# Evacuations after both halves of a split, one tile sum later, and an earlier turn in the mixer

## The chip, the cores and the metric

The kernel runs on one core of a Trainium2 chip. The metric is the device time of one launch in microseconds, and lower is better. The kernel before took 2287.01 us (median of 3 runs, 2286.39 to 2288.19).

The names of the engines in the profile: PE is TensorE (matmuls; PEld is its weight load), DVE is VectorE, ACT is ScalarE, POOL is GpSimd, SP is SyncE, which here only issues DMA transfers.

## The reference

A sequence of 256 tokens with 2048 features passes through two blocks, all in fp32. The part that fills most of the time is the MLP of the first block, which is computed twice, with other weights:

```python
for i in range(DEPTH):                     # DEPTH = 2
    h = rmsnorm(x, g[0])
    m = hyena_shortconv_mixer(h, ...) if i % 2 == 0 else pool_mixer(h, ...)
    x = x + rmsnorm(m, g[1])
    h = rmsnorm(x, g[2])
    f = jnp.square(jax.nn.relu(h @ mlp_w1[i])) @ mlp_w2[i]   # 2048 -> 8192 -> 2048
    x = x + rmsnorm(f, g[3])
```

The mixer of the first layer begins with `z = h @ w_in` (2048 by 6144, `in_w_z` in the trace). A third layer with three kinds of attention follows, and a last rmsnorm. The change doesn't touch it.

## The kernel before

**Products.** A weight tile is 128 by 2048 fp32 (1024 KB). A product of fp32 operands is made of three fp32r matmuls: each operand is split into a high part and the rest, and PE adds hi by hi, hi by low and low by hi into one PSUM bank (`product`, L353). The high part of a weight tile is an ACT copy (L497, `hi<-raw`), the low part a DVE subtraction (L616, `low<-raw,hi`). Each tile is split in two halves of 128 by 1024, so a tile costs ACT two copies and DVE two subtractions. PE waits for the low part of a tile's half before it begins that half's matmuls.

**Buffers.** There are 3 landing buffers (raw0 to raw2) and 3 pairs of operand buffers (hi and low, 0 to 2). SP loads tiles in the order in which they are used. A load waits until its landing buffer is free, and loads behind it on SP's queue wait as well.

**The order.** The order of all work is written out by hand: the function `conduct` runs once for each engine, and each engine keeps what is its own. Before a tile is used (`take`), the tiles up to two further on are split; after its last product (`release`) the one behind these, if an operand pair is free. `release` has an argument `between`, which is called between the two halves of that split. The evacuation of a finished PSUM bank is put there, so on ACT and DVE the order is: first half, evacuation, second half.

**The MLP.** A chunk is 1024 of the 8192 hidden features. The first goes up on its own; for each of the other 7 (e = 1 to 7, so 14 in both MLPs) `both_ways` interleaves the way up for chunk e with the way down for chunk e-1. The way up is done with 7 half-size products in place of 8 (a Strassen scheme in Winograd's form), each of 2 weight tiles: up(1) to up(7). The way down is 8 tiles of `w_d`, down(0) to down(7). A tile on the way up has 12 matmuls, one on the way down 24 (two banks). So a chunk is 22 tiles, in this order (numbers of the tiles in the chunk in brackets):

up(1) (0, 1), down(0) (2), up(2) (3, 4), down(1) (5), up(5) (6, 7), down(2) (8), up(3) (9, 10), down(3) (11), up(6) (12, 13), down(4) (14), up(7) (15, 16), down(5) (17), up(4) (18, 19), down(6) (20), down(7) (21).

**Tile sums.** The operands of the 7 products are sums of weight tiles. They are made in a chain in the buffers R_f and X (two tiles each). POOL issues accumulating DMAs into R_f (L1008), DVE adds two tiles with `tile_sum` (L601): `first_sum`, R_f<-R_f,X, and `third_sum(0)` and `third_sum(1)`, X<-X,raw. The third sums read the tiles of up(3) (9 and 10) where they have landed. They stand in the middle of down(2), and each also frees the landing buffer of its tile: only then does SP load the next tile of `w_d` into it. The buffer that third_sum(1) frees takes the tile of down(5), and the loads for down(6) and down(7) stand behind it on SP. X, the result, holds the tiles of up(7) (15 and 16).

**Evacuations in the MLP.** The end of up(6), `sixth`, is the long one: DVE combines two products (L601, `EV<-P,EV` twice, two banks), then ACT takes relu (L553) and square (L555) of the second. The ends of the odd down tiles add two banks to R_m on DVE (`summed`, L601, R_m<-P,R_m); for e = 1 they are copies on ACT.

**The mixer.** `gemm` computes 512 columns of `in_w_z` for two banks with 4 tiles. When one is done, the banks are evacuated to EV (ACT, L492), and four transposes on PE, a turn (L356, P<-ident,EV), bring a quarter of it into another layout. Turns stand in a list `later`, from which one entry is taken after each half tile; entries `nop` only put off what is behind them.

## Time and profile before

| | |
|---|---|
| median of 3 runs | 2287.01 us (2286.39 to 2288.19) |
| profiled execution, its time | 2288.19 us |
| its span in the trace | 2286.4 us |
| PE busy | 2265.3 us (99%), 10609 matmuls |
| PE weight load busy | 1874.1 us (82%) |
| DVE busy | 1724.9 us (75%) |
| ACT busy | 1325.8 us (58%) |
| POOL busy | 81.0 us (4%) |
| DMA | 513.26 MB, mean 224 GB/s |

The profiled execution is the slowest of the three. Its own time is 1.8 us over its span, 2288.19 less 2286.4, for what lies before the first and behind the last instruction. Idle time of an engine other than PE costs something only where PE waits for it. "Granted clock" or PEclk is the share of full speed that the throttle granted TensorE; 1.00 is 2.4 GHz.

### The profile page before, as it was taken

The numbers are of one execution on the slowest core, as the hardware profiler recorded it, in microseconds if no ns is written. First come the engines' busy times: TensorE is split into PE (matmuls) and PEld (weight loads), VectorE is DVE, ScalarE is ACT, GpSimd is POOL, SyncE is SP. The second block draws the span as 40 slices with busy tenths as digits, with TensorE's granted clock in tenths as the row PEclk, the third lists the DMA queues.
The fourth block names the chain that finished last, engine by engine and source line by source line (L and its number), as shares of the span: only waits on it lengthen the run. The fifth ranks groups of instructions, "written<-read, shape, count | busy, mean of one in ns | idle before, by whom it ended". The sixth has DMA issues, their size and how long they took to land.

```text
span 2286.4 us, 26583 instructions
## 1 busy us (share of the span) xinstructions
PE 2265.3 (99%) x10609; PEld 1874.1 (82%) x10609; DVE 1724.9 (75%) x2043; ACT 1325.8 (58%) x1769; POOL 81.0 (4%) x110
## 2 busy tenths in 40 slices
PE   9999999999999999999999999999999999999998
PEld 7778788878888888888887888888888888888887
DVE  6675864888788788887878888888878775456664
ACT  6444444666666766665666666666666564444453
POOL 0000000000000000000000000000000010000000
PEclk9999999999999999999999999999999999999999
DMA  9444455787797797786576797797688645654443
GB/s 351 168 165 169 160 187 184 272 242 226 256 283 236 251 282 229 258 265 239 224 288 188 247 286 219 242 290 223 241 272 239 232 159 200 246 187 148 147 157 120
DMA packets 73100, 513.26 MB, mean 224 GB/s; under 512 B 8234, under 2 KB 8565, under 8 KB 13520
## 3 DMA queue, kind: packets, MB, share of 16 engines
q1 hardware_dynamic: 61568, 429.58, 50.4%
q0 software_dynamic: 11264, 81.87, 16.0%
q8 instruction: 84, 1.38, 0.2%
q14 instruction: 40, 0.32, 0.0%
q10 hardware_dynamic: 144, 0.12, 0.0%
HBM read 505.24 MB, written 6.29 MB: 224 GB/s over the span
## 4 chain that ended last, share of the span: by engine, by line
PE 93%; DVE 3%; DMA 2%; ACT 1%; issue 1%; POOL 0%; SPq 0%; ACTq 0%; POOLq 0%; DVEq 0%
PE P L353 90%; PE P L356 3%; DVE low L616 2%; DMA raw<-in_w_d 1%; ACT hi L497 1%; DVE R_f L601 0%; DMA raw<-in_w_z 0%; DVE R_m L601 0%; DVE X L604 0%; DVE R_f_r L601 0%; ACT EV L523 0%; DVE R_h L604 0%; DVE R_g_r L601 0%; ACT R_m L492 0%; DVE st L604 0%
## 5 line engine op out<-in xcount | busy, mean ns | idle before, releaser
L616 DVE TENSOR_TENSOR low<-raw,hi 128x1024 fp32r<-128x1024 f32 (+3 forms) x694 | 813.2, 1199 | 281.8 <-ACT hi L497 277.6
L497 ACT ACTIVATE hi<-raw 128x1024 fp32r<-128x1024 f32 (+3 forms) x694 | 705.1, 1040 | 471.9 <-PE P L353 334.5
L353 PE MATMUL P<-hi,R_h 128*128 128x512 f32 (+2 forms) x2944 | 948.8, 394 | 1.7 <-DVE low L616 1.2
L353 PE MATMUL P<-hi,R_f_r 128*128 128x512 f32 x2480 | 793.7, 392 | 7.0 <-DVE low L616 6.7
L353 PEld LDWEIGHTS P<-hi,R_h 128*128 128x128 f32 x2944 | 553.3, 188 | 119.9 <-issue 8.6
L353 PE MATMUL P<-low,R_h 128*128 128x512 f32 (+2 forms) x1472 | 570.9, 388 | 0.0
L353 PEld LDWEIGHTS P<-hi,R_f_r 128*128 128x128 f32 x2480 | 467.2, 188 | 106.2 <-DVE low L616 8.0
L353 PE MATMUL P<-low,R_f_r 128*128 128x512 f32 x1240 | 484.0, 390 | 0.0
L353 PEld LDWEIGHTS P<-low,R_h 128*128 128x128 f32 x1472 | 277.2, 188 | 56.3 <-issue 4.3
L616 DVE TENSOR_TENSOR low<-R_f,hi 128x1024 fp32r<-128x1024 f32 x226 | 265.0, 1219 | 70.1 <-ACT hi L497 70.1
L353 PEld LDWEIGHTS P<-low,R_f_r 128*128 128x128 f32 x1240 | 233.6, 188 | 47.4
L497 ACT ACTIVATE hi<-R_f 128x1024 fp32r<-128x1024 f32 x226 | 230.7, 1052 | 60.0 <-PE P L353 30.2
L353 PE MATMUL P<-hi,R_g_r 128*128 128x512 f32 x448 | 142.4, 389 | 0.0
L553 ACT ACTIVATE EV<-EV,st 128x512 f32<-128x512 f32 x42 | 30.4, 724 | 120.8 <-DVE EV L601 120.8
L353 PEld LDWEIGHTS P<-hi,R_g_r 128*128 128x128 f32 x448 | 84.1, 188 | 17.4
L616 DVE TENSOR_TENSOR low<-X,hi 128x1024 fp32r<-128x1024 f32 x56 | 67.9, 1223 | 37.3 <-ACT hi L497 35.6
L353 PE MATMUL P<-low,R_g_r 128*128 128x512 f32 x224 | 87.1, 389 | 0.0
L1008 POOL DMA_DIRECT2D R_f<-in_w_u x56 | 48.6, 868 | 1013.0 <-DVE low L616 1013.0
L601 DVE TENSOR_TENSOR R_m<-P,R_m 128x512 f32<-128x512 f32 x112 | 71.9, 683 | 6.1 <-PE P L353 6.1
L353 PE MATMUL P<-hi,R_s_r 128*128 128x512 f32 x224 | 71.4, 390 | 0.0
L356 PE MATMUL P<-ident,EV 128*128 128x128 f32 (+1 forms) x476 | 66.4, 272 | 0.0
L497 ACT ACTIVATE hi<-X 128x1024 fp32r<-128x1024 f32 x56 | 58.8, 1057 | 11.4 <-PE P L353 11.4
(221 smaller groups left out, 1453.9 us busy)
## 6 DMA issues: line engine op xcount, KB each, us to landing
raw<-in_w_d SPq DMA_DIRECT2D x128, 1024.0 KB, 5.9
raw<-in_w_u SPq DMA_DIRECT2D x72, 1024.0 KB, 5.1
R_f<-in_w_u POOLq DMA_DIRECT2D x56, 1024.0 KB, 12.0
raw<-in_w_z SPq DMA_DIRECT2D x45, 1024.0 KB, 4.9
raw<-in_w_i SPq DMA_DIRECT2D x36, 1024.0 KB, 4.8
R_f<-in_w_u SPq DMA_DIRECT2D x28, 1024.0 KB, 6.6
X<-in_w_u SPq DMA_DIRECT2D x28, 1024.0 KB, 8.2
raw<-in_w_mo SPq DMA_DIRECT2D x16, 1024.0 KB, 4.9
```

Source lines behind the costliest of these rows:

```text
L353: return self.e.matmul(o, l, r, start=start, stop=stop, skip_group_check=True)
L356: return self.e.transpose(o, i, self.m.ident[0:i.shape[0], 0:i.shape[0]])
L497: self.e.activation(hi, raw, ACT.Copy).then_inc(*self.inc("high_made", ("high", k, d)))
L553: self.e.activation(o, p, ACT.Relu, scale=r).then_inc(*self.inc("act_done", evacuated))
L601: self.e.tensor_tensor(o, a, b, op).then_inc(*self.inc("dve_done", *done))
L616: self.e.tensor_tensor(low, raw, hi.bitcast(f32), ALU.subtract).then_inc(*self.inc("low_made", *lows))
L1008: self.e.dma_start(o, i, accum_op=ALU.add).then_inc(*self.landed(f"added{j}", done))
```

## The change

Three edits.

1. `between` is gone. `release` now splits both halves of the next tile and the evacuation comes behind them. The ends of up(6) and up(4) are called with `soon`, and there the evacuation comes first and both halves behind it.
2. `third_sum(1)` moves from the middle of down(2) to up(6), behind the `take` of its first tile (12). `third_sum(0)` stays.
3. In the mixer, the number of `nop` entries ahead of the turns of product 0 is 2 in place of 4, and none in place of 1 for product 1.

No instruction is added or removed. On SP and POOL the order of the instructions is the same in both kernels.

```diff
--- before.py
+++ after.py
@@ -1111,21 +1111,16 @@
 
     chain_last = [None] * 4
 
-    def split_ahead(n, between=None):
+    def split_ahead(n):
         while not listing and not at_["pause"] and at_["high"] < min(at_["load"], n):
             k = at_["high"]
             o = plan[k][7]
             if o is not None:
                 if o >= NO and o - NO not in used:
-                    break
+                    return
                 split_part(k, 0, 2)
-                if between is not None:
-                    between()
-                    between = None
                 split_part(k, 1, 2)
             at_["high"] += 1
-        if between is not None:
-            between()
 
     def quarters():
 
@@ -1160,7 +1155,7 @@
             return j, m.raw[l % NL][0:parts, 0:c]
         return j, m.hi[o % NO][0:parts, 0:c], m.low[o % NO][0:parts, 0:c]
 
-    def release(j, done, hold=False, between=None):
+    def release(j, done, hold=False):
         l, o = plan[j][6:8]
         if o is None:
             freed[l] = done
@@ -1168,7 +1163,7 @@
             used.add(o)
         load_ahead()
         if not hold:
-            split_ahead(j + 2 + AHEAD, between)
+            split_ahead(j + 2 + AHEAD)
 
 
     bank_free, bank_held = [[] for _ in range(8)], set()
@@ -1741,7 +1736,7 @@
         if n == 7:
             flush_all()
         ks, ms = evac(banks, done, scale_m=list(r1_m))
-        later += [nop] * {0: 4, 1: 1, 8: 1, 9: 1, 10: 1}.get(n, 0)
+        later += [nop] * {0: 2, 8: 1, 9: 1, 10: 1}.get(n, 0)
         for c in (0, 2):
             later.append(lambda kind=kind, c=c + 4 * (n % 2), ks=ks, ms=ms: mixer_turn(kind, c, ks, ms))
         if n == 7:
@@ -1863,7 +1858,7 @@
         def parts_of(n, *free):
             s_m[n] = plain_parts(SH[n], SL[n], SUM[n], [s_m[n], list(free)])
 
-        def half_product(b, xh, xl, ready, tiles, end, onto, aside):
+        def half_product(b, xh, xl, ready, tiles, end, soon, onto, aside):
 
             for n, tile in enumerate(tiles):
                 j, wh, wl = take(up_w, *tile)
@@ -1875,10 +1870,13 @@
                     whose = ([("product", j, 1)] if k == 3 else []) + ([("used", j, k // 2)] if k % 2 else [])
                     E.product(P[b][:, :], xh[:, 4 * n + k, :], xl[:, 4 * n + k, :], wh[:, k, :], wl[:, k, :], j, k,
                               onto is None and n == k == 0, n == 1 and k == 3, x, bank_free[b], *whose)
-                done = "product", j, 1
-                release(j, done, between=(lambda: end(b, done)) if n == 1 else None)
+                if n == 1 and soon:
+                    end(b, ("product", j, 1))
+                release(j, ("product", j, 1))
+                if n == 1 and not soon:
+                    end(b, ("product", j, 1))
                 step()
-            return done
+            return ("product", j, 1)
 
         def down_tile(e, i, banks, middle):
             g, q = i // 2, i % 2
@@ -1895,7 +1893,10 @@
                 if k == 1:
                     middle()
             done = ("product", j, 1)
-            release(j, done, between=(lambda: [summed(e, t, g, banks[t], done) for t in range(2)]) if q == 1 else None)
+            release(j, done)
+            if q == 1:
+                for t in range(2):
+                    summed(e, t, g, banks[t], done)
             step()
             return done
 
@@ -1970,8 +1971,8 @@
             h_left, h_right = list(h_m[0:8]), list(h_m[8:16])
             up_done = {}
 
-            def up(n, b, xh, xl, ready, tiles, end, onto=None, aside=nop):
-                up_done[n] = half_product(up_banks[b], xh, xl, ready, tiles, end, onto, aside)
+            def up(n, b, xh, xl, ready, tiles, end, soon=False, onto=None, aside=nop):
+                up_done[n] = half_product(up_banks[b], xh, xl, ready, tiles, end, soon, onto, aside)
 
             def down(i, middle=nop):
                 return down_tile(e - 1, i, down_banks, middle)
@@ -1984,14 +1985,14 @@
             up(2, 0, HH[:, HRIGHT, TOP], HL[:, HRIGHT, TOP], h_right, plain(b21), second, onto=ms[1], aside=lambda: first_sum(1))
             down(1)
             up(5, 1, SH[1], SL[1], s_m[1], linked(1), fifth)
-            down(2, lambda: [third_sum(j) for j in range(2)])
+            down(2, lambda: third_sum(0))
             up(3, 1, SH[4], SL[4], s_m[4], plain(b22, "kept"), third, onto=ms[5])
             down(3)
-            up(6, 0, SH[2], SL[2], s_m[2], linked(2), sixth)
+            up(6, 0, SH[2], SL[2], s_m[2], linked(2), sixth, True, aside=lambda: third_sum(1))
             down(4)
             up(7, 0, SH[3], SL[3], s_m[3], linked(4), seventh)
             down(5)
-            up(4, 1, HH[:, HRIGHT, BOTTOM], HL[:, HRIGHT, BOTTOM], h_right, linked(3), fourth)
+            up(4, 1, HH[:, HRIGHT, BOTTOM], HL[:, HRIGHT, BOTTOM], h_right, linked(3), fourth, True)
             left_free = down(6)
             right = [(c, *turned(c, right_ks(), right_ms())) for c in (4, 6)]
```

On DVE, in the middle of the first chunk, around down(2) (raw1 and raw2 in the rows with X hold tiles 9 and 10):

```order
 L616 TENSOR_TENSOR low1<-raw2,hi1 128x1024 x2
 L601 TENSOR_TENSOR X<-X,raw1 128x2048
-L601 TENSOR_TENSOR X<-X,raw2 128x2048
 L616 TENSOR_TENSOR low2<-raw0,hi2 128x1024 x2
 L616 TENSOR_TENSOR low0<-R_f,hi0 128x1024 x2
```

The second sum has left this place; the first is where it was.

On DVE in the same chunk, from up(6) on (`low0<-X` is the split of tile 15, `low1<-X` that of tile 16, `EV0<-P2,EV0` and `EV3<-P3,EV0` are the two combinations at the end of up(6)):

```order
 L616 TENSOR_TENSOR low2<-raw1,hi2 128x1024 x2
 L601 TENSOR_TENSOR R_h<-R_m,R_h 128x8x128
+L601 TENSOR_TENSOR X<-X,raw2 128x2048
 L616 TENSOR_TENSOR low0<-X,hi0 128x1024 x2
-L616 TENSOR_TENSOR low1<-X,hi1 128x1024
 L601 TENSOR_TENSOR EV0<-P2,EV0 128x512
 L601 TENSOR_TENSOR EV3<-P3,EV0 128x512
-L616 TENSOR_TENSOR low1<-X,hi1 128x1024
```

The sum now stands right ahead of the splits of tiles 15 and 16, and the first half of tile 16 has moved from the front of the two combinations to their back (the two halves follow there as `L616 TENSOR_TENSOR low1<-X,hi1 128x1024 x2`).

On DVE in the second chunk, from down(3) on, before (`low0<-raw1` is the split of tile 14, `R_m<-P0,R_m` and the next the evacuation of down(3)):

```order
L616 TENSOR_TENSOR low0<-raw1,hi0 128x1024
L601 TENSOR_TENSOR R_m<-P0,R_m 128x512
L601 TENSOR_TENSOR R_m<-P1,R_m 128x512
L616 TENSOR_TENSOR low0<-raw1,hi0 128x1024
L616 TENSOR_TENSOR low1<-X,hi1 128x1024 x2
L616 TENSOR_TENSOR low2<-X,hi2 128x1024
L601 TENSOR_TENSOR EV4<-P2,EV4 128x512
L601 TENSOR_TENSOR EV1<-P3,EV4 128x512
L616 TENSOR_TENSOR low2<-X,hi2 128x1024
```

and now:

```order
L616 TENSOR_TENSOR low0<-raw1,hi0 128x1024 x2
L601 TENSOR_TENSOR R_m<-P0,R_m 128x512
L601 TENSOR_TENSOR R_m<-P1,R_m 128x512
L601 TENSOR_TENSOR X<-X,raw2 128x2048
L616 TENSOR_TENSOR low1<-X,hi1 128x1024 x2
L601 TENSOR_TENSOR EV4<-P2,EV4 128x512
L601 TENSOR_TENSOR EV1<-P3,EV4 128x512
L616 TENSOR_TENSOR low2<-X,hi2 128x1024 x2
```

The later chunks have the same order with other buffers.

On PE in the mixer, at the first turn of product 0 (P6<-ident,EV4), before:

```order
L353 MATMUL P0<-hi0,R_h 128x512
L353 MATMUL P1<-hi0,R_h 128x512
L353 MATMUL P1<-low0,R_h 128x512
L353 MATMUL P1<-hi0,R_h 128x512
L356 MATMUL P6<-ident,EV4 128x128
L356 MATMUL P6<-ident,EV5 128x128
```

and now:

```order
L353 MATMUL P0<-hi2,R_h 128x512
L353 MATMUL P1<-hi2,R_h 128x512
L353 MATMUL P1<-low2,R_h 128x512
L353 MATMUL P1<-hi2,R_h 128x512
L356 MATMUL P6<-ident,EV4 128x128
L356 MATMUL P6<-ident,EV5 128x128
```

The turn stands one tile, 24 matmuls, earlier, in the tile whose operands are hi2 and low2.

## Rows read from the trace of the kernel before

**Rows 1.** waits of PE over the span: engine, line, tile waited for, total, times, longest.

```profile
PE P L353 <- DVE low L616: 7.9, 5, 3.1
PE P L356 <- DVE X L604: 2.7, 3, 1.6
```

**Rows 2.** stretches by engine: length, PE, PEld, DVE, ACT, POOL busy (count), PEclk, DMA share, GB/s.

```profile
900.00:1000.00 100.00, 100.00 (x451) 82.97 (x450) 85.52 (x77) 62.78 (x69) 3.75 (x5) 1.00 0.82 260
490.00:505.00 15.00, 11.96 (x46) 9.41 (x45) 12.57 (x11) 10.85 (x13) 1.72 (x2) 0.89 0.96 295
829.00:844.00 15.00, 14.46 (x64) 11.63 (x63) 14.85 (x15) 10.03 (x11) 1.75 (x2) 1.00 0.97 263
40.00:55.00 15.00, 14.07 (x65) 10.77 (x64) 10.49 (x9) 10.39 (x12) 0.00 (x0) 1.00 0.94 347
1840.00:1855.00 15.00, 12.77 (x64) 11.27 (x63) 12.84 (x38) 8.54 (x26) 4.46 (x5) 0.89 0.22 76
```

**Rows 3.** chain of waits, 480 to 494 us: start, length, what.

```profile
480.23 11.02 DMA raw<-in_w_d
491.27 1.06 ACT hi L497
492.36 1.24 DVE low L616
```

**Rows 4.** timeline of PE, matmuls behind idle time: start, length, operation [idle before].

```profile
42.01 0.50 PE L353 MATMUL P<-hi,R_h 128*128 128x512 f32 x1 [0.93 <-DVE low L616]
...
493.64 0.67 PE L353 MATMUL P<-hi,R_f_r 128*128 128x512 f32 x1 [3.04 <-DVE low L616]
...
830.40 0.50 PE L353 MATMUL P<-hi,R_f_r 128*128 128x512 f32 x1 [0.54 <-DVE low L616]
...
1843.51 1.32 PE L356 MATMUL P<-ident,X 128*128 128x128 f32 x8 [1.59 <-DVE X L604]
```

**Rows 5.** timeline of DVE, 484 to 515 us.

```profile
484.66 4.48 DVE L601 TENSOR_TENSOR X<-X,raw 128x2048 f32<-128x2048 f32 x2
...
506.24 3.49 DVE L616 TENSOR_TENSOR low<-X,hi 128x1024 fp32r<-128x1024 f32 x3
509.64 1.41 DVE L601 TENSOR_TENSOR EV<-P,EV 128x512 f32<-128x512 f32 x2
513.46 1.23 DVE L616 TENSOR_TENSOR low<-X,hi 128x1024 fp32r<-128x1024 f32 x1 [2.40 <-ACT hi L497]
```

**Rows 6.** timeline of ACT, 511 to 513 us.

```profile
511.08 0.72 ACT L553 ACTIVATE EV<-EV,st 128x512 f32<-128x512 f32 x1 [4.23 <-DVE EV L601]
511.84 0.63 ACT L555 ACTIVATE EV<-EV 128x512 f32<-128x512 f32 x1
```

**Rows 7.** timeline of PE, first matmuls of tile 16, chunks 1 and 2.

```profile
514.18 0.62 PE L353 MATMUL P<-hi,R_h 128*128 128x512 f32 x2
...
597.60 0.61 PE L353 MATMUL P<-hi,R_h 128*128 128x512 f32 x2
```

**Rows 8.** timeline of DVE, chunk 2, end of down tile 3.

```profile
584.42 1.29 DVE L601 TENSOR_TENSOR R_m<-P,R_m 128x512 f32<-128x512 f32 x2 [0.23 <-PE P L353]
```

**Rows 9.** DMA, 583 to 587.5 us: the queue's share; issues with KB and us to landing.

```profile
q0 software_dynamic: 102, 0.84, 92.6%
R_f<-in_w_u POOLq DMA_DIRECT2D x1, 1024.0 KB, 13.0
raw<-in_w_d SPq DMA_DIRECT2D x1, 1024.0 KB, 10.5
```

**Rows 10.** DMA issues of the whole page: times, KB each, median us to landing.

```profile
raw<-in_w_d SPq DMA_DIRECT2D x128, 1024.0 KB, 5.9
```

**Rows 11.** timeline of ACT, 38 to 40 us.

```profile
38.48 1.27 ACT L492 ACTIVATE EV<-P,st 128x512 f32<-128x512 f32 x2 [1.98 <-PE P L353]
```

**Rows 12.** timeline of PE, 37 to 45 us.

```profile
37.97 0.62 PE L353 MATMUL P<-hi,R_h 128*128 128x512 f32 x2
...
44.86 0.60 PE L356 MATMUL P<-ident,EV 128*128 128x128 f32 x4
```

## The prediction

> **What bounds the kernel.** I read the page's busy shares first: PE is busy for 2265.3 of 2286.4 us, so all its idle time is 21.1 us, and no order of work can gain more than that without fewer matmuls. The waits of PE show who makes it idle: the low parts (DVE, L616) five times, 7.9 us in all, and sums of X three times, 2.7 us [rows 1]. The stretches show the steady state: from 900 to 1000 us PE is busy for 100.00 us at a granted clock of 1.00, 451 matmuls, 0.222 us each (0.227 in the timeline, where no record is missing); DVE is busy for 86% beside it and DMA for 82% [rows 2]. So DVE has some slack on average, and a change of order costs or gains only where one of its chains ends later than PE's next tile.
>
> The largest wait is 3.04 us at 493.64 [rows 4], in the first chunk of the first MLP; one of the same kind stands in the second MLP. The chain shows its cause: the load for down(3)'s tile is issued at 480.23 and takes 11.02 us beside POOL's accumulating loads, then the high part 1.06, the low part 1.24 [rows 3]. From landing to PE's start that is 493.64 - 491.25 = 2.39 us.
>
> Idle time can cost twice, through the clock. The 15 us around the 3.04 us wait have a granted clock of 0.89, as have those around the wait of 1.59 us at 1843.51; those around 0.54 us (830.40) and 0.93 us (42.01) have 1.00 [rows 2, 4]. At 0.89 over 15 us, 15 x 0.11 = 1.65 us are lost on top of the wait. So PE dropped to a lower clock behind waits of 1.6 us and more, did not behind 0.93, and nothing in the trace lies between.
>
> **The mixer's earlier turn.** The turn at 44.86 [rows 12] moves 24 matmuls forward, to where PE is at 38.19 (the second of the pair at 37.97), and needs the evacuation that ACT makes from 38.48 to 39.75 [rows 11]. PE is through with the matmul before it at about 38.36 and now waits until 39.80: 1.44 us. The wait of 0.93 at 42.01, for a low part, goes in exchange, since PE comes there later (39.80 + about 0.4 for four transposes + 12 matmuls, 2.72: 42.9). Net 1.44 - 0.93 = 0.5, less 0.1 for the slow first matmul behind a wait (0.50 against 0.39): +0.4 us. The other turns move up where their evacuation is long done; I cost them at nothing, hidden by the matmuls between, and bound them by -0.5 and +0.5.
>
> **The evacuation behind both halves.** DVE and ACT do the same work. What moves is the low part of a second half, 1.2 us earlier, and the evacuation, 1.2 us later. An earlier split gains only where PE waits for it, or where it frees a landing buffer for a load that is late. The late load is that of down(3): its buffer is freed by a low part that in the first chunk may now come up to 0.6 us earlier, as an ACT copy of 0.6 no longer stands in it. Since the landing depends on the accumulating loads as well, I take 0.3 of 0 to 0.6, once in each MLP: -0.6. The later evacuation costs nothing if its bank is not needed: down(3)'s ends at 584.42 + 1.29 = 585.71 before [rows 8] and about 587.95 now, and down(4) begins two up tiles behind, 584.4 + 2 x 2.72 = 589.8. Without this cover each would cost up to 1.2 us.
>
> **The third sum behind up(6)'s start.** It takes 2.24 us (two in 4.48) [rows 5]. In its old place in the first chunk DVE stood idle before down(3) anyway, so nothing is gained by taking it away. In its new place it stands ahead of the chain that feeds tile 16:
> - first chunk, before: two lows of tile 15 and one of 16 from 506.24, two combinations 509.64 to 511.05 [rows 5], relu 511.08, square 511.84 to 512.47 [rows 6], high part, low part 513.46 to 514.69 [rows 5].
> - now: sum 506.24 to 508.5, two lows to 510.7 (one less ahead), two combinations to 512.12, and then relu, square, high and low of the first half, the same 514.69 - 511.05 = 3.64 us as before, to 515.76. PE wants tile 16 at 514.41, the second matmul of the pair at 514.18 [rows 7]. Before, the first half was ready in time; now PE waits 515.76 - 514.41 = 1.35, with the semaphore 1.4 us. The order on ACT is what does it: the high part of 16's first half is now queued behind relu and square, and these behind the combinations. Also tight: the first combination frees its bank at 511.40 and PE wants it at 511.69.
> - second chunk: the sum is behind down(3)'s evacuation: 587.95 + 2.2 = 590.15, two lows to 592.42, two combinations to 593.75, + 3.64 = 597.4. PE wants it at 597.83 [rows 7]. That is 0.4 us in time. The later chunks have the same order; I cost them at nothing, and the cover is 0.4 us thin.
>
> So the wait comes once in each MLP: 2 x 1.4 = +2.8. The bounds are 0 (if the lows run 1.4 us ahead of what I laid out) and, for all 14 chunks, what the third rival below takes.
>
> The sum also issues later, and with it a transfer: the load of down(5)'s tile waits for it. In the second chunk it is issued at 590.2, about 15 us later, and the loads for down(6) and down(7) stand behind it on SP, so they go together. PE wants down(5)'s tile at 597.83 + 2.72 = 600.55, so it must land by 600.55 - 2.39 = 598.2, within 8.0 us. The median is 5.9 [rows 10], but a load beside the accumulating ones took 10.5 (and the accumulating one 13.0) [rows 9]. I take 6.5 (near the median, since the accumulating load issued shortly after 583 has had the queues to itself until then), and so no cost; the bounds are 0 and 2.5 us a chunk. Between them: the load beside the accumulating one lost 4.6 us in 10.5, 0.44 for each us of overlap. If the accumulating load still lands at about 583.4 + 13.0 = 596.4, the new load overlaps it for 6.2 us and loses 2.7: it lands at 598.8, 0.6 us late.
>
> The Trainium skill says ("DMA: Bandwidth & Descriptors", section "Queues, rings and completion order") that a DMA engine goes round between the queues that have work, packet by packet, so that a load beside another gets about every other turn. The trace agrees roughly: 10.5 beside an accumulating load against a median of 5.9, with that queue at 92.6% of the engines' share [rows 9, 10]. By this rule the new issue pays for its overlap alone, half of it: 6.2 us until the accumulating load's end would add 3.1 us, PE would wait 1.0 us in each of 12 chunks, and the sum would be 12 us higher.
>
> **Sum.** +0.4 (mixer) + 2.8 (tile 16) - 0.6 (down(3)) = +2.6 us. The three new waits are 1.44, 1.3 and 1.3 us as idle time, between the 0.93 that kept the clock and the 1.59 that lost it. Each costs 0 to 1.65 us more; the bounds are 0 and 5.0. I take one of three, as they are nearer to 1.59: +1.65, together +4.2. Against the profiled execution (span 2286.4, 1.8 around it, 2288.19) that is 2292.4; this execution is 1.2 us over the median, so for the median 2287.01 + 4.2 = 2291.2. A change of 0.2% is 4.6 us, and less can't be told from none here: the bounds are 2282.4 and 2291.6.
>
> **Rivals.**
> - No new waits of weight: the splits run ahead of my layout, tile 16 is in time, down(3)'s load gains its whole 0.6. 0.4 - 1.2 = -0.8, and with half of the mixer's term 2286 to 2287. For it: DVE is idle for 2.40 us in this stretch [rows 5]. Against: this idle time is spent in just the chain that gets longer.
> - Slower by over 0.2%, the tile sum in all chunks: the 0.4 us of cover in the later chunks is used up by one more queued split or a load that comes late. The point from which it decides is a low part of tile 16 later than PE's 0.4 us; if the chain is 1.0 us longer than laid out, 0.6 x 12 = 7.2 more, 2287.0 + 2.6 + 7.2 = 2296.8. For it: one operation out of place on DVE is 1.2 us. Against: the same durations gave a layout of before that fits its rows.
> - Slower by over 0.2%, down(5)'s load: at the measured 10.5 us it lands at 600.7, and PE waits 2.5 us, in 12 chunks 30 us, 2287.0 + 2.6 + 30 = 2320. With the overlap worked out above it is 12 x 0.6 = 7.2 more: 2296.8. Against both: nothing else of SP is under way between 583.5 and 590.2.
> - Faster: down(3)'s load comes early enough that PE keeps its clock, and tile 16 is in time: 2 x (0.6 + 1.65) = 4.5 less 0.4 for the mixer, 2282.9. Against: 3.04 - 0.6 = 2.4 is still more than 1.59.
>
> **Chances.** The forecast 0.45 (own range 2289.6 with no clock step to 2294.5 with all), no new waits 0.22, the sum in all chunks 0.17, down(5)'s load 0.08 (of which 0.03 by the overlap), faster 0.08. Of the forecast's 0.45, 0.27 lies below 2291.6. So faster by over 0.2% 0.08; within 0.2% 0.22 + 0.27 = 0.49; slower 0.18 + 0.17 + 0.08 = 0.43. The range 2284.5 to 2300 leaves out the fastest and the slow load, 0.16.
>
> **What would show it.** In the profile after: a new wait of 1.2 to 1.5 us of PE for the low part in tile 16 near 515 us, and again in the second MLP, none in the later chunks; a wait of about 1.4 us for the evacuation near 38.4 us and none near 42; the wait for down(3)'s tile at 2.4 to 3.0 us; the sum X<-X,raw in the second chunk ending near 590 us, and the load behind it landing before 598. Stretches of 15 us around each wait say by PEclk, 1.00 or 0.89, who pays for the clock. It is wrong if tile 16 isn't waited for, or if there are waits of 0.3 us and more in most of the 12 later chunks.

## The result and the profile after

The changed kernel takes 2310.95 us (median of 5 runs, 2309.43 to 2312.64) against 2287.01 us (5 runs): a ratio of 1.0103 (95% interval 1.0089 to 1.0118), 24 us slower. The forecast was 2291.2 us with a range up to 2300. The direction of its sum was right, its size was a sixth of what was measured.

The profiled execution took 2310.16 us, 22.0 us more than that of before, and so did its span (2308.4 against 2286.4). PE is idle for 37.3 us of it instead of 21.1, and is "busy" for 5.8 us more, in matmuls slowed at the restart behind a wait and by the clock. The waits of PE in the changed kernel, as in [rows 1] (total, times, longest):

```profile
PE P L353 <- DVE R_m L601: 12.9, 12, 1.4
PE P L353 <- DVE low L616: 8.7, 6, 3.6
PE P L356 <- ACT EV L492: 3.0, 2, 1.6
```

The first row is what the forecast doesn't have: 12 waits, one in each chunk but the first of each MLP, for an evacuation R_m<-P,R_m. It is that of down(5), and PE waits for its bank ahead of down(6). (The kernel before has a single one, 0.18 us at 695.41.) The third row is the mixer: two waits for an evacuation, where one was forecast.

PE's timeline has the first matmul behind each wait. Rows from the mixer (two), the end of the mixer's block, the first MLP's first chunk (down(3)'s tile, then tile 16), down(3)'s tile in the second MLP, and a down(6):

```profile
39.90 0.63 PE L356 MATMUL P<-ident,EV 128*128 128x128 f32 x4 [1.56 <-ACT EV L492]
...
59.58 0.63 PE L356 MATMUL P<-ident,EV 128*128 128x128 f32 x4 [1.40 <-ACT EV L492]
...
404.33 0.99 PE L356 MATMUL P<-ident,X 128*128 128x128 f32 x5 [0.75 <-DVE X L604]
...
496.25 0.80 PE L353 MATMUL P<-hi,R_f_r 128*128 128x512 f32 x1 [3.49 <-DVE low L616]
...
518.55 0.50 PE L353 MATMUL P<-hi,R_h 128*128 128x512 f32 x1 [0.16 <-DVE low L616]
...
1264.07 0.79 PE L353 MATMUL P<-hi,R_f_r 128*128 128x512 f32 x1 [3.59 <-DVE low L616]
...
1554.48 0.47 PE L353 MATMUL P<-hi,R_f_r 128*128 128x512 f32 x1 [1.23 <-DVE R_m L601]
```

and two of before that answer to the third and the sixth:

```profile
402.20 0.99 PE L356 MATMUL P<-ident,X 128*128 128x128 f32 x5 [0.75 <-DVE X L604]
...
1250.62 0.50 PE L353 MATMUL P<-hi,R_f_r 128*128 128x512 f32 x1 [3.15 <-DVE low L616]
```

With [rows 4] this gives where the time comes in. To 404.33 the changed kernel is 2.1 us behind (402.20 before): the mixer. From there to 1264.07 it needs 859.7 us instead of 848.4 (to 1250.62), +11.3: the first MLP, and the second up to down(3)'s tile. To the transposes at 1866.72 (1843.51 before) it needs 602.7 instead of 592.9, +9.8: the rest of the second MLP. From there on it gains 1.2 us. So all but the mixer's 2.1 us lies in the MLPs. The wait for tile 16, on which half of the forecast's sum rested, is 0.16 us.

The granted clock around the waits (columns as in [rows 2]):

```profile
490.00:505.00 15.00, 11.51 (x39) 9.00 (x38) 9.96 (x9) 7.02 (x8) 1.72 (x2) 0.77 0.58 159
38.00:53.00 15.00, 13.44 (x62) 10.39 (x61) 8.97 (x11) 10.08 (x13) 1.97 (x4) 1.00 0.92 336
1546.00:1561.00 15.00, 13.77 (x65) 11.21 (x65) 10.09 (x12) 8.28 (x10) 0.00 (x0) 1.00 0.97 384
```

The mixer's wait of 1.56 us and the wait of 1.23 us at 1554.48 leave it at 1.00. Around the 3.5 us ahead of down(3) it is 0.77 (0.89 before).

The chain of waits shows how a later sum becomes a wait 25 us behind it. This is the chain that ends at PE's wait at 1554.48 (start, length, what):

```profile
1528.41 1.20 DVE R_m L601 x2
1529.61 2.21 DVE X L601
...
1531.84 7.71 DMA raw<-in_w_d
...
1539.57 1.07 ACT hi L497
...
1540.66 6.90 DVE low L616 x6
...
1547.57 0.61 DVE EV L601
...
1548.27 0.70 DVE EV L601
...
1549.00 0.74 ACT EV L553
...
1550.29 1.05 ACT hi L497
...
1551.37 2.36 DVE low L616 x2
1553.73 0.61 DVE R_m L601
...
1554.48 0.70 PE P L353 x2
```

It goes from the evacuation of down(3) through the sum (2.21) and the load of down(5)'s tile (7.71) to that tile's high part. ACT waited 0.84 us for the load, so the sum's queue on DVE and ACT would have brought it here nearly as late:

```profile
1539.57 2.01 ACT L497 ACTIVATE hi<-raw 128x1024 fp32r<-128x1024 f32 x2 [0.84 <-DMA raw<-in_w_d]
```

From 1540.66 on DVE and ACT have no pause that isn't one's wait for the other: six low parts (tiles 17, 18, 19), the two combinations of up(7)'s end, relu and square on ACT, then the high and low parts of tile 20, and only then the evacuation that PE waits for. The timeline of DVE has the same with the idle time:

```profile
1540.66 2.36 DVE L616 TENSOR_TENSOR low<-raw,hi 128x1024 fp32r<-128x1024 f32 x2 [0.49 <-ACT hi L497]
1542.94 4.62 DVE L616 TENSOR_TENSOR low<-R_f,hi 128x1024 fp32r<-128x1024 f32 x4
1547.48 0.69 DVE L601 TENSOR_TENSOR EV<-P,EV 128x512 f32<-128x512 f32 x1
1548.27 0.69 DVE L601 TENSOR_TENSOR EV<-EV 128x512 f32<-128x512 f32 x1
1551.37 2.36 DVE L616 TENSOR_TENSOR low<-raw,hi 128x1024 fp32r<-128x1024 f32 x2 [2.41 <-ACT hi L497]
1553.65 1.28 DVE L601 TENSOR_TENSOR R_m<-P,R_m 128x512 f32<-128x512 f32 x2
```

The 2.41 us are the stretch in which relu, square and a high part stand on ACT. In the kernel before, the same stretch of the same chunk was:

```profile
1519.62 2.35 DVE L616 TENSOR_TENSOR low<-raw,hi 128x1024 fp32r<-128x1024 f32 x2
1521.89 2.35 DVE L616 TENSOR_TENSOR low<-R_f,hi 128x1024 fp32r<-128x1024 f32 x2
1524.40 1.23 DVE L616 TENSOR_TENSOR low<-R_f,hi 128x1024 fp32r<-128x1024 f32 x1 [0.16 <-ACT hi L497]
1525.54 0.68 DVE L601 TENSOR_TENSOR EV<-P,EV 128x512 f32<-128x512 f32 x1
...
1529.42 1.23 DVE L616 TENSOR_TENSOR low<-R_f,hi 128x1024 fp32r<-128x1024 f32 x1 [2.40 <-ACT hi L497]
1530.57 1.22 DVE L616 TENSOR_TENSOR low<-raw,hi 128x1024 fp32r<-128x1024 f32 x1
1531.70 1.28 DVE L601 TENSOR_TENSOR R_m<-P,R_m 128x512 f32<-128x512 f32 x2
1532.90 3.49 DVE L616 TENSOR_TENSOR low<-raw,hi 128x1024 fp32r<-128x1024 f32 x3
```

There the combinations (1525.54) don't wait for tile 19's second half, and the evacuation (1531.70) doesn't wait for tile 20's. The pair of evacuations ended at 1532.98, and down(6) began at 1535.3, 2.3 us behind it. The slack is 0.45 us more, 2.75, since PE only waits for the first of the two banks: in the changed kernel it began at 1554.48, 0.45 us ahead of the pair's end at 1554.93. From tile 17's first low part to the evacuation it took 1531.70 - 1519.62 = 12.1 us, now 13.0. So 0.9 us go to the new order, 2.2 to the sum and 0.8 to the lateness of the load: 3.9 us, less 2.75 of slack, leave 1.15, and the wait is 1.23.

### The profile page after: what moved, and what is told of

Its sections match the earlier page's. It is cut to its first block, busy times and chain, and to the rows that moved or that the text cites. A ratio compares the mean times of both kernels' runs of the same rounds, so it can differ in the third digit from the quotient of the medians.

```text
span 2308.4 us, 26572 instructions
## 1 busy us (share of the span) xinstructions
PE 2271.1 (98%) x10609; PEld 1874.3 (81%) x10609; DVE 1718.6 (74%) x2043; ACT 1316.3 (57%) x1769; POOL 80.9 (4%) x110
## 3 DMA queue, kind: packets, MB, share of 16 engines
q0 software_dynamic: 11264, 81.87, 15.8%
## 4 chain that ended last, share of the span: by engine, by line
PE 77%; DVE 13%; DMA 5%; ACT 3%; issue 1%; POOL 0%; ACTq 0%; POOLq 0%; DVEq 0%
PE P L353 74%; DVE low L616 8%; DMA raw<-in_w_d 5%; PE P L356 3%; ACT hi L497 2%; DVE R_m L601 1%; DVE X L601 1%; DVE EV L601 1%; ACT EV L553 1%; DVE R_f L601 0%; ACT R_h L492 0%; DVE R_f_r L601 0%; DVE R_h L604 0%; DVE X L604 0%; DVE R_h L601 0%
## 5 line engine op out<-in xcount | busy, mean ns | idle before, releaser
L616 DVE TENSOR_TENSOR low<-raw,hi 128x1024 fp32r<-128x1024 f32 (+3 forms) x694 | 810.3, 1201 | 376.7 <-ACT hi L497 373.7
L353 PE MATMUL P<-hi,R_f_r 128*128 128x512 f32 x2480 | 797.7, 394 | 21.4 <-DVE R_m L601 12.9
L616 DVE TENSOR_TENSOR low<-R_f,hi 128x1024 fp32r<-128x1024 f32 x226 | 261.8, 1220 | 31.3 <-ACT hi L497 31.3
L497 ACT ACTIVATE hi<-R_f 128x1024 fp32r<-128x1024 f32 x226 | 223.6, 1048 | 47.1 <-DVE R_f L601 29.6
L616 DVE TENSOR_TENSOR low<-X,hi 128x1024 fp32r<-128x1024 f32 x56 | 66.0, 1222 | 33.6 <-ACT hi L497 33.6
L356 PEld LDWEIGHTS P<-ident,EV 128*128 128x128 f32 (+1 forms) x476 | 56.5, 139 | 12.5 <-ACT EV L492 1.9
```

Source lines behind the costliest of these rows:

```text
L353: return self.e.matmul(o, l, r, start=start, stop=stop, skip_group_check=True)
L356: return self.e.transpose(o, i, self.m.ident[0:i.shape[0], 0:i.shape[0]])
L497: self.e.activation(hi, raw, ACT.Copy).then_inc(*self.inc("high_made", ("high", k, d)))
L616: self.e.tensor_tensor(low, raw, hi.bitcast(f32), ALU.subtract).then_inc(*self.inc("low_made", *lows))
```

## The experiments

All times are medians, each beside that of the kernel before, run at the same time (it lay between 2284.93 and 2287.37 us, so the ratios are what compares).

| kernel | us | kernel before | ratio (95% interval) |
|---|---|---|---|
| mixer's edit alone | 2289.45 | 2287.37 | 1.0009 (0.9999 to 1.0018) |
| sum's move alone | 2296.05 | 2287.37 | 1.0043 (1.0029 to 1.0058) |
| order of evacuations alone | 2286.80 | 2287.37 | 0.9997 (0.9988 to 1.0007) |
| order + an extra DVE pass | 2301.16 | 2287.37 | 1.0063 (1.0048 to 1.0078) |
| changed, R_m first at a down tile's end | 2296.58 | 2285.93 | 1.0051 (1.0036 to 1.0066) |
| changed, up(7)'s end first | 2310.55 | 2285.93 | 1.0109 (1.0094 to 1.0124) |
| order + sum, mixer as before | 2308.25 | 2285.93 | 1.0095 (1.0079 to 1.0112) |
| order + load held back | 2303.27 | 2285.93 | 1.0079 (1.0064 to 1.0094) |
| order + sum in down(3) | 2310.65 | 2284.93 | 1.0113 (1.0098 to 1.0128) |
| before, an add held back | 2291.80 | 2284.93 | 1.0029 (1.0017 to 1.0040) |
| changed, POOL's loads plain (leaves out the additions to R_f) | 2291.83 | 2285.52 | 1.0029 (1.0017 to 1.0040) |
| mixer with 3 entries | 2286.1 (one run) | 2284.93 | |

### The three edits one by one

The mixer's table alone:

```diff
-        later += [nop] * {0: 4, 1: 1, 8: 1, 9: 1, 10: 1}.get(n, 0)
+        later += [nop] * {0: 2, 8: 1, 9: 1, 10: 1}.get(n, 0)
```

> The kernel before with the third edit alone (2 nop entries ahead of the turns of product 0, none for product 1). The trace of the changed kernel has two new waits of PE for the evacuation in the mixer, 1.56 us at 39.90 and 1.40 us at 59.58, and the wait of 0.93 us is gone; from the end of the mixer's first part on, its matmuls start 2.15 us later than before. If the three edits don't act on each other, this kernel takes 2.1 us more than before (2289). If the earlier turns give something back further on, 0 to 1 us more.

+2.1 us, as expected, though the interval of the ratio (-0.2 to 4.1 us) doesn't exclude zero. The traces do: the transposes at the end of the mixer's block begin at 403.4 to 404.3 us in the five kernels with this edit, and at 401.2 to 402.5 in the nine without. Its trace has waits of 1.77 us at 39.60 and 1.40 us at 59.30. The first is the one that was forecast (1.44); it was 0.22 to 1.77 us in the five traces, as PE comes there sooner or later by its waits in the first 11 us. The second comes from product 1, whose single entry is gone too: there the turn's evacuation isn't done either, and I had costed it at nothing.

The sum's move alone:

```diff
-            down(2, lambda: [third_sum(j) for j in range(2)])
+            down(2, lambda: third_sum(0))
-            up(6, 0, SH[2], SL[2], s_m[2], linked(2), sixth)
+            up(6, 0, SH[2], SL[2], s_m[2], linked(2), sixth, aside=lambda: third_sum(1))
```

> The kernel before with the second edit alone: third_sum(1) behind the take of tile 12, each evacuation still between the halves of a split. Theory A (the queue of DVE): the sum makes all that is behind it on DVE about 3 us later, and with the order of before the evacuation of down(5) ends about 1.1 us earlier than in the changed kernel. So PE waits about 0.3 us or not at all ahead of down(6), 0 to 6 us in 12 chunks, and the whole is 1 to 9 us slower than before. Theory B (the sum alone does it, by the load of down(5)'s tile that it holds back): waits of 1.0 to 1.3 us as in the changed kernel, 15 to 20 us slower. Theory C (the new order of evacuations does it): no waits, within 2 us of before.

+8.7 us, within what theory A gave. But its waits are not those that theory A named: for R_m there are only two of 0.2 us, where the kernel before has one. The waits that are new or longer are single ones for low parts of other tiles (1.18 us at 686.32, 1.50 at 833.71, 0.52 at 856.32), one of 1.01 at 1048.94 for a sum into R_f_r, and 0.8 us in each first chunk for the first combination's bank (at 511.70 and 1275.47). The forecast had called this bank tight (0.3 us). At down(6) the slack is nearly gone, but it holds: the pair of evacuations ends between 0.23 us ahead of PE's start and 0.45 behind it. So this run hit the number for another reason. With no waits of 1.0 us for R_m, theory B is out.

The order alone (`True` in the calls of up(6) and up(4) is not shown):

```diff
+                if n == 1 and soon:
+                    end(b, ("product", j, 1))
                 release(j, ("product", j, 1))
+                if n == 1 and not soon:
+                    end(b, ("product", j, 1))
...
             release(j, done)
+            if q == 1:
+                for t in range(2):
+                    summed(e, t, g, banks[t], done)
```

> The kernel before with the first edit alone: both halves of a split ahead of the evacuation, and up(6) and up(4) with the evacuation first; third_sum(1) stays in down(2), the mixer as before. Theory A (both edits are needed): the evacuation of down(5) ends about 0.5 us before PE wants its bank, no waits ahead of down(6), within 2 us of before. Theory B (the sum alone): the same, no waits. Theory C (the order alone): waits of 1.0 to 1.3 us ahead of down(6) in the 12 later chunks, 15 to 20 us slower.

No change, and no wait for R_m: theory C is out. The pair ends 0.6 to 0.96 us ahead of PE's start at down(6) in nine of the 12 chunks, and in three 0.45 us behind it, just in time. Sum and order apart come to 8.7 - 0.6 = 8.1 us. Together, with the mixer as before, they should then take 2294, and don't:

> The changed kernel with the mixer as before: the first two edits. The mixer's edit alone cost 2.1 us. If it doesn't act on the others, 2309 (2308 to 2310). If its later start shifted the MLP against the loads, more than 1.5 us off that.

+22.3 us. The mixer's edit is additive within the noise; the sum and the order are not. 14 us of the 24 are in neither of the two edits but in both at once: each alone fits into the 2.75 us of slack at down(6), and together they don't.

### Which part of the sum: its time on DVE or the load behind it

The sum does two things where it stands: it takes 2.28 us of DVE, and it holds a load back. First the DVE time alone. Both sums stay in down(2), and a pass of the same size stands in the new place, which leaves its data as they are:

```diff
+            def extra_pass():
+                E.tile_pass(m.chain[3], [("chained", l, e, 4, 1)], ("passed", l, e))
...
-            up(6, ..., sixth, True, aside=lambda: third_sum(1))
+            up(6, ..., sixth, True, aside=extra_pass)
```

> Both third sums in down(2) as before, so that the load of down(5)'s tile is issued as early as before, and the new order of evacuations. Added is one more DVE pass of the size of the sum (X<-X,X, 128x2048, maximum with itself, which changes nothing) in the place where the change puts the sum. It tells the sum's time on DVE from the load that the sum holds back. Theory A (DVE's queue): the waits for R_m ahead of down(6) come as in the changed kernel, 0.6 to 1.3 us each, at most 0.8 us shorter where the load was late; 8 to 20 us slower than before. Theory B (the held-back load): no such waits, 0 to 3 us slower. In both, the first chunk waits for down(3)'s tile as before.

+13.8 us, and a very regular trace:

```profile
PE P L353 <- DVE R_m L601: 7.6, 12, 0.6
```

```profile
1461.37 0.47 PE L353 MATMUL P<-hi,R_f_r 128*128 128x512 f32 x1 [0.63 <-DVE R_m L601]
...
1545.69 0.47 PE L353 MATMUL P<-hi,R_f_r 128*128 128x512 f32 x1 [0.64 <-DVE R_m L601]
```

Each of the 12 waits is 0.64 us, and a chunk takes 1545.69 - 1461.37 = 84.32 us instead of 597.60 - 514.18 = 83.42 [rows 7]. So a wait of 0.64 costs 0.90: 0.26 go to the slower matmuls at the restart.

Now the load alone. The sums stay in down(2), but the landing buffer is given free by a DVE operation of 128x8 elements in the new place:

```diff
-                if not listing:
+                if not listing and j == 0:
                     freed[landed] = done
                     load_ahead()
+            def free_late():
+                landed, done = None if listing else plan[kept_at + 1][6], ("passed", l, e)
+                E.tile_pass(m.chain[3][:, 0:8], [("chained", l, e, 4, 1)], done)
+                if not listing:
+                    freed[landed] = done
+                    load_ahead()
```

> The new order of evacuations, both third sums in down(2) on DVE as before, but the landing buffer of the second sum is only given free in the place where the change has the sum, by a DVE operation of 128x8 elements. So the load of down(5)'s tile is held back as in the change, without the sum's 2.28 us on DVE in that place. With the extra pass alone (no held-back load) each of the 12 waits was 0.64 us; in the changed kernel 0.64 to 1.35. Theory A (mostly DVE's queue, the load adds to it only because the chain has no slack left): waits for R_m of 0 to 0.3 us, at most 5 us slower than before (2287 to 2292). Theory B (the held-back load by itself costs what the changed kernel has more than the one with the pass): waits of 0.4 to 0.7 us, 6 to 10 us slower than before.

+17.3 us, with 11 waits for R_m up to 1.4: both theories had it too low, A by far. The held-back load costs as much as the sum's time on DVE and more. The two don't add up: 13.8 and 17.3 alone, 22.3 together. ACT's timeline shows it waiting for the load of down(5)'s tile (1617.65), and the issues say why. Three rows of this kernel: the wait, then the later accumulating load (issued at 1603.5) and the load of w_d (issued at 1608.1), KB and us to landing:

```profile
1617.65 2.01 ACT L497 ACTIVATE hi<-raw 128x1024 fp32r<-128x1024 f32 x2 [2.69 <-DMA raw<-in_w_d]
```

```profile
R_f<-in_w_u POOLq DMA_DIRECT2D x1, 1024.0 KB, 12.8
...
raw<-in_w_d SPq DMA_DIRECT2D x1, 1024.0 KB, 9.6
```

The first lands at 1603.5 + 12.8 = 1616.3, the second at 1608.1 + 9.6 = 1617.6. In the kernel before, the same load was issued ahead of the accumulating ones and took 6.1 us (issued at 1499.2).

### Where the load may stand

If the load is late, an earlier sum should help. The sum moves into down(3), a tile and a half earlier:

```diff
-            down(3)
+            down(3, lambda: third_sum(1))
-            up(6, ..., sixth, True, aside=lambda: third_sum(1))
+            up(6, ..., sixth, True)
```

> The first two edits (mixer as before), with third_sum(1) in the middle of down(3) in place of up(6): one tile and a half earlier. On DVE it stands ahead of the split of tile 14 and of the evacuation of down(3), and the load of down(5)'s tile is issued about 5 us earlier than in the change, but nearer to the accumulating loads. With the sum in up(6) it took 2308 us. If the chain from the split of down(5)'s tile to the evacuation of down(5) (about 14 us on DVE) is what is late, it now starts 0.8 to 1.3 us earlier in each chunk, since tile 17 waits neither for the sum nor for its load, and most of the 12 waits go: 2288 to 2298. If the order of evacuations alone set the waits, they stay: 2304 to 2310.

A miss: +25.7 us, slower than with the sum in up(6). PE waits 13.7 us for R_m (11 times) and 17.0 us for low parts (14 times; 10.7 and 8 with the sum in up(6)). The issue is earlier (1527.25 in the same chunk, against 1531.84), but now it stands right behind the accumulating loads of 1523.0 and 1525.3. Their later one, and the load of w_d:

```profile
R_f<-in_w_u POOLq DMA_DIRECT2D x1, 1024.0 KB, 14.2
...
raw<-in_w_d SPq DMA_DIRECT2D x1, 1024.0 KB, 12.4
```

Issued 4.6 us earlier, it lands at 1527.25 + 12.4 = 1539.7; in the changed kernel 1531.84 + 7.71 = 1539.6, where the accumulating load was issued at 1525.5 and took 12.5. So in the three chunks shown the load lands 0.1 to 1.6 us behind the accumulating one, and 14.1 to 14.3 us after that one's issue: when it was issued itself hardly matters here. The accumulating load pays for an early one (14.2 us in place of 12.5). In the other chunks of the changed kernel in which it is issued 5.6 to 7.6 us behind, it lands 1.3 to 2.4 us behind, once 3.7; with the sum in down(3), issued 1.9 us behind, it lands within 0.3 us behind in all the others but one, where it lands 1.0 ahead. The wait for down(3)'s tile in [rows 3] has the same cause. Holding back the accumulating load there, in the kernel before:

```diff
         if s in (1, 2):
+            if (e, s, j) == (1, 1, 1) and mlp_ in ahead_of:
+                free = [free, ("loaded", ahead_of[mlp_])]
```

> The kernel before with one more wait: in the first chunk of each MLP the second accumulating load of up(6)'s operand is only issued when the tile of down(3) has landed. It tells what the 3.0 us wait of PE there, once in each MLP, is made of. If the load is late because it shares the engines with that accumulating load, it lands about 4 us earlier, PE doesn't wait for down(3)'s tile and keeps its clock: 2 x (3.04 + 1.65) = 9.4 us less, and the accumulating load comes later, with 0 to 3 us of wait and perhaps a clock loss at tile 13 in exchange: 2279 to 2287. If the load is slow for another reason: 2286 to 2290, with the wait of 3 us where it was.

The mechanism is partly confirmed: the load of down(3)'s tile, issued at 479.33, now takes 5.6 us instead of 11.0, and the wait of 3.0 us at down(3) is gone. The time doesn't: +6.9 us, since the accumulating load is now late for its own tile (0.82 us at 498.73 and 3.88 at 1260.15), and the load of down(4)'s tile behind it for that (2.91 at 504.65, 1.41 at 1266.07). So here the wait was only moved. The engines' share was 0.96 in this stretch before [rows 2]; whether another order could do without the wait was not run.

Another run takes the accumulation away. In the changed kernel POOL's loads are plain, so its result is not the reference's:

```diff
-        self.e.dma_start(o, i, accum_op=ALU.add).then_inc(*self.landed(f"added{j}", done))
+        self.e.dma_start(o, i).then_inc(*self.landed(f"added{j}", done))
```

> The changed kernel with the 56 accumulating loads of POOL as plain loads of the same tiles: the addition to R_f is left out, so the operands of up(6) and up(4) aren't the sums. In all kernels so far a load of w_d that is issued beside the accumulating loads lands 0.2 to 1.5 us behind the later one of them, whenever it was issued. Theory D (the load of down(5)'s tile and the sum on DVE are two chains that end at the split of tile 17, and the load is held by the accumulating loads): the load now lands in 5 to 7.5 us, only the sum's 2.28 us on DVE is left, and each of the 12 waits for R_m falls to 0.64 us as with the extra pass alone; the waits of 3.5 us for down(3)'s tile and their clock loss go (2 x 4.7), the first chunk waits for tile 16 instead (2 x 1.3). 2311 - 12 x 0.5 - 9.4 + 2.4 = 2298 (2294 to 2302). If the load is slow for its own queue (three loads of w_d are issued at once), the waits stay over 1.0 us: 2301 to 2306 with the gain at down(3) alone.

Its waits of PE, and the issues of the later POOL load and of down(5)'s tile in one chunk:

```profile
PE P L353 <- DVE R_m L601: 7.7, 12, 0.6
...
PE P L353 <- DVE low L616: 2.4, 2, 1.3
```

```profile
R_f<-in_w_u POOLq DMA_DIRECT2D x1, 1024.0 KB, 5.2
...
raw<-in_w_d SPq DMA_DIRECT2D x1, 1024.0 KB, 4.9
```

The load takes 4.9 us, and each wait for R_m is 0.64 us, within 0.01 of what the extra pass alone gave. So theory D holds: at tile 17's split two chains meet, the sum on DVE (worth 0.64 us of wait) and the load held behind the accumulating loads (the rest: nothing in two of the 12 chunks, 0.3 to 0.7 us in the others). The rival that the load is slow for the two loads of w_d issued right behind it is out as the whole cause: they are here too. But POOL's plain load has landed before they are issued, so this run doesn't tell what part they have in the delay when all share the engines. The waits for low parts fall from 8.7 to 2.4 us, the first chunk's for down(3)'s tile being gone. The time is 6 us below what I expected and below its range too, 2291.8 for 2298. I had priced the waits at down(3) by the clock of before (0.89), and in the changed kernel it was 0.77: 2 x 15 x 0.12 = 3.6 us of the six. The two waits for low parts at 838.13 and 860.66 (1.3 us) are gone as well.

### Which part of the order

Two runs move one evacuation each to the front in the changed kernel. First that of the down tiles:

```diff
-            release(j, done)
             if q == 1:
                 for t in range(2):
                     summed(e, t, g, banks[t], done)
+            release(j, done)
```

> The changed kernel with one line moved: at the end of an odd down tile the two additions R_m<-P,R_m come first and both halves of the split behind them. Theory A (DVE's queue: the evacuation of down(5) is late because it stands behind the split of down(6)'s tile, whose high part stands on ACT behind relu and square of up(7)'s end): the bank is free 2.3 us earlier, the 12 waits for R_m (12.9 us, and about 0.25 us each at restart, 16 us in all) go; low parts of tile 20 come 1.2 us later, at about the moment PE wants them, so 0 to 0.6 us come back in each chunk as waits for low. 8 to 16 us faster than the changed kernel: 2295 to 2303. Theory B (the held-back load limits the whole chain): the waits turn into waits for low of the same size, 2308 to 2312.

12 us faster than the changed kernel by the ratios (1.0051 and 1.0103), 14 by the medians, and no wait for R_m is left. One line decides the 12 waits. Low parts of tile 20 come in time. What remains, besides the mixer, is one wait of 1.18 us at 1048.56 for a sum into R_f_r, three for low parts of 0.16 to 0.32, and the first chunks: the 3.4 us for down(3)'s tile, and now a wait for tile 16 of 1.28 and 1.26 us:

```profile
517.67 0.50 PE L353 MATMUL P<-hi,R_h 128*128 128x512 f32 x1 [1.28 <-DVE low L616]
...
1279.21 0.50 PE L353 MATMUL P<-hi,R_h 128*128 128x512 f32 x1 [1.26 <-DVE low L616]
```

This is the wait that was forecast (1.3 us of idle time), in its place. The changed kernel has it at 0.16 us because PE there ran at the lower clock behind down(3) and came about a microsecond later. The other traces bear this out: with the first two edits alone, and with up(7)'s end first, it is 1.19 and 1.28 us in the first MLP, where the clock around down(3) was 0.89, and 0.16 in the second, where it was 0.77.

Then the end of up(7):

```diff
-            up(7, 0, SH[3], SL[3], s_m[3], linked(4), seventh)
+            up(7, 0, SH[3], SL[3], s_m[3], linked(4), seventh, True)
```

> The changed kernel with the end of up(7) ahead of both halves of its split, as up(6) and up(4) have it. Theory A: relu and square of up(7)'s end are then out of the way on ACT before the high part of tile 20; the combinations move about 4.6 us forward on DVE, the splits of tile 19 move 1.4 us back, and the evacuation of down(5) ends 1 to 2 us earlier: the 12 waits for R_m go or fall under 0.3 us. 10 to 16 us faster than the changed kernel: 2295 to 2301. Theory B (the held-back load): nothing changes, 2308 to 2312.

A miss for theory A: no change. The 12 waits stay (11.3 us). The number is theory B's, but the run before this one rules B out: there the waits went without the load being any earlier. The combinations moved from behind tile 19's low parts to their front, but DVE's idle time of 2.40 us behind relu and square moved with them, and the evacuation stands behind the same work as before. On this chain the order of what lies ahead didn't count, only what was taken out from ahead.

### The mixer with 3 entries

> The kernel before with 3 nop entries ahead of the turns of product 0, in place of 4 (the change has 2 and also takes the one of product 1). The first turn then stands where PE is at 40.9, behind the end of its evacuation at 39.75, so there is no wait for the evacuation, and the wait for the low part at 42.01 shrinks from 0.93 by the 0.4 of the turn: 0.4 us less than before in the mixer, nothing else. If the two waits of the changed mixer (1.56 and 1.40) come from each turn's place alone, neither shows here.

As expected: no wait for an evacuation, and none at 42. But the absence at 42 shows nothing: that wait is 0.38 to 1.0 us in the other traces with the mixer as before, and missing in one of them as well (the first two edits). The profiled span was 2284.3; 0.4 us is below what one run can tell.

## Why the prediction was wrong

- **What bounds the kernel** held: PE is busy all the time but for its waits, and these say where time is lost.
- **The mixer.** The first turn waited 1.56 us for 1.44; the same turn's wait is 0.22 to 1.77 us in five traces, so a hit this close is in part luck. The step that the other turns cost nothing failed for product 1: its first turn waits 1.40 us. +2.1 instead of +0.4.
- **The first chunk.** DVE's layout to tile 16 was right: where the rest left it alone, PE waits 1.2 to 1.3 us (down(5)'s order first, extra pass, plain loads). In the changed kernel the clock loss ahead of it hid the wait. The gain of 0.3 us at down(3) didn't come; that wait was 3.49 and 3.59 us. The buffer was freed earlier, and the load issued 2.0 us behind the accumulating load's issue in place of 2.6, but it took 12.1 us in place of 11.0 and landed 0.2 us behind that load, as before (first MLP; 12.2 in place of 11.1 in the second).
- **The later chunks: the step that failed.** I followed the chain behind the sum to tile 16, found 0.4 us of cover, and stopped. That part was right: there is no wait for tile 16 in the 12 later chunks. But the chain goes on, through the splits of tiles 17 to 20, up(7)'s end and down(5)'s evacuation. All of it is later by the sum's 2.2 us too, and with the order and the load that evacuation is 3.9 us later on a slack of 2.75. "The later evacuation costs nothing if its bank is not needed" I had tested at down(3) alone, not at down(5), where the same edit and the sum meet. 12 waits, 12.9 us, and 0.26 us more at each restart, 3.1: 16 of the 22 us of the profile, where the forecast had nothing.
- **The load of down(5)'s tile** was taken at 6.5 us and out of the way of the accumulating load, which would have had the queues to itself. In that chunk it was issued at 594.5 and took 7.1 us, in most later ones 7.4 to 7.8. This was the rival "down(5)'s load", in a mild form: measured alone it costs more than the sum's time on DVE. But PE waited for that tile itself only once (0.48 us at 860.66); the lateness reached it through the same evacuation. A price for each us of overlap is a poor form: the load lands shortly behind the accumulating one, so its length follows from how early it is issued. By the Trainium skill's rule of turns between queues ("DMA: Bandwidth & Descriptors", section "Queues, rings and completion order") a load that gets every other turn would take, as an estimate, twice the 4.9 us of the run with plain loads, 9.8 us. The trace of the kernel with the sum in down(3) shows 12.4. From 1527.3 to 1539.5 the queue of the accumulating load moved 236 packets and SP's queue 213, so the turns were about even; but the first took 68.5% of the engines' time and the second 32.3%, so an accumulating turn was about twice as long as a plain one. SP's 213 packets were 1.61 MB, more than the one load, so the loads behind it had part of its turns. The 92.6% that the prediction set beside the rule [rows 9] is of a stretch in which SP's queue moved 4 packets, and says nothing of turns.
- **The clock.** I placed a threshold between waits of 0.93 and 1.59 us. Waits of 1.56, 1.40 and 1.0 to 1.36 us all left the clock at 1.00, so nothing was lost there. The very wait of 1.59 us on which the threshold rested, with 0.89 at 1843.51, is there in the changed kernel too (1866.72), with 1.00. At down(3)'s tile a wait of 3.08 us went with 0.77 (the mixer with 3 entries), 3.31 with 1.00 (the mixer's edit alone), and waits of 2.5 to 3.6 with 0.89: no length of wait settled it, and what does stays open. The step from 0.89 to 0.77 at down(3) in both MLPs is, by the same product, 2 x 15 x 0.12 = 3.6 us more. With the 16 and the mixer's 2.1 this makes 21.7 of the 22 us; other waits are 2 us longer together, and the clock kept at 1866.72 gives about as much back.
- **The rivals.** "The tile sum in all chunks" named the right mechanism (a chain on DVE that outgrows its cover in the 12 later chunks) at the wrong place, with 7.2 us for the 16. The range ended at 2300 and left all beyond it to the slow load.

## What to carry to other kernels

When an edit delays an operation on an engine, follow that engine's queue until a stretch of idle time swallows the delay, not to the first consumer that is still in time; here that stretch lay behind a bank four tiles on. Slack is spent once: here two edits that cost 0 and 9 us apart cost 22 us together, so test them together where they draw on the same slack. And a load that would be issued beside accumulating loads is to be placed by when those land, not by its usual length.

## What the runs showed of the hardware

- In the chunks shown, a 1024 KB load issued 1.9, 4.5 and 6.4 us behind an accumulating load of the same size took 12.4, 9.6 and 7.7 us and landed 0.1 to 1.6 us behind it. With plain loads, no longer beside each other, both take 4.9 to 5.2 us in that place.
- With the same bytes, that queue's share of the engines falls from 15.8% (changed kernel) to 9.6% (plain loads): so much of it is the accumulation.
- Waits of PE of 0.6 to 1.6 us, new in the changed kernel (12 ahead of down(6), two in the mixer), left its granted clock at full speed. One of 1.59 us, in both kernels, went with 0.89 before and 1.00 after. Waits of 3.3 to 3.6 us for down(3)'s tile gave 0.77 over 15 us in the changed kernel, and with the order alone 0.89 in the first MLP (3.31 us) and 1.00 in the second (3.53). So the length of the wait alone didn't set the clock.
